# The vector engine's order in the first feed-forward layer: remainders of a later step, and reads of a finished product

## What is computed

```python
hn = rms_norm(h, p['norm_ff_g'])                      # h: 1280 x 1024
ff = jnp.square(jax.nn.relu(hn @ p['w_ff1'])) @ p['w_ff2']   # w_ff1: 1024 x 4096, w_ff2: 4096 x 1024
return h + ff
```

## Time and profile before

| | us |
|---|---|
| median of 3 runs | 2267.54 (2267.01 to 2267.8) |
| the profiled execution, its own time | 2268.52 |
| its span, from the first instruction to the last | 2266.8 |
| PE busy | 2212.8 (98% of the span) |
| PE weight loads busy | 1995.3 (88%) |
| DVE busy | 1438.4 (63%) |
| ACT busy | 1069.5 (47%) |

### The profile page before, as it was taken

How to read it: one execution, slowest core, us unless ns; L and a number is a source line. 1 busy time by engine, 2 the same in 40 slices (tenths; PEclk the granted TensorE clock), 3 DMA queues, 4 the chain that set the end, 5 groups by cost and what they waited for, 6 DMA issues and landing times.

```text
span 2266.8 us, 35228 instructions
## 1 busy us (share of the span) xinstructions
PE 2212.8 (98%) x13706; PEld 1995.3 (88%) x13706; DVE 1438.4 (63%) x2196; ACT 1069.5 (47%) x1870; POOL 166.0 (7%) x284
## 2 busy tenths in 40 slices
PE   8999999899998999999899999999999999999999
PEld 6888888788886888888788888899999999999999
DVE  6333455467653666677777645477676777786776
ACT  7533322266665444566633333365555654444442
POOL 0000000111100000000000000011111112111110
PEclk9999999999999999999999999999999999999999
DMA  4333322555545776888775243465555479887886
GB/s 163 109 118 135 114 95 81 143 137 158 137 126 161 237 229 220 264 260 264 229 256 168 87 157 106 150 208 195 177 200 195 159 249 355 297 288 251 275 289 235
DMA packets 227980, 434.92 MB, mean 192 GB/s; under 512 B 16355, under 2 KB 132963, under 8 KB 223116
## 3 DMA queue, kind: packets, MB, share of 16 engines
q1 hardware_dynamic: 188652, 321.71, 43.0%
q0 software_dynamic: 39200, 111.45, 16.2%
HBM read 331.93 MB, written 103.27 MB: 192 GB/s over the span
## 4 chain that ended last, share of the span: by engine, by line
PE 48%; DVE 2%; DMA 0%; issue 0%; ACT 0%; DVEq 0%
PE acc L150 13%; PE acc L148 13%; PE acc L149 13%; PE late_acc L148 3%; PE late_acc L149 3%; PE late_acc L150 3%; DVE xn_lo L1885 0%; DMA merged<-s_y_T 0%; DVE h_T L2597 0%; DVE hn_plain L2571 0%; DVE hn_plain L2580 0%; DVE ff_w_s L2588 0%; DVE gates L2006 0%; DVE ff_far_t_lo L2539 0%; DVE w_lo L2534 0%
## 5 line engine op out<-in xcount | busy, mean ns | idle before, releaser
L148 PE MATMUL acc<-xn_hi,w_hi 128*128 128x512 f32 (+1 forms) x1176 | 420.9, 358 | 22.8 <-DVE xn_lo L617 10.7
L149 PE MATMUL acc<-xn_hi,w_lo 128*128 128x512 f32 (+1 forms) x1176 | 418.4, 356 | 0.0
L150 PE MATMUL acc<-xn_lo,w_hi 128*128 128x512 f32 (+1 forms) x1176 | 417.6, 355 | 0.0
L148 PE MATMUL late_acc<-xn_hi,w_hi 128*128 128x512 f32 (+1 forms) x768 | 286.5, 373 | 3.0 <-DVE late_result_a L867 1.9
L148 PEld LDWEIGHTS acc<-xn_hi,w_hi 128*128 128x128 f32 x1176 | 223.5, 190 | 57.7 <-issue 13.6
L150 PE MATMUL late_acc<-xn_lo,w_hi 128*128 128x512 f32 (+1 forms) x768 | 274.2, 357 | 0.0
L149 PE MATMUL late_acc<-xn_hi,w_lo 128*128 128x512 f32 (+1 forms) x768 | 273.3, 356 | 0.0
L150 PEld LDWEIGHTS acc<-xn_lo,w_hi 128*128 128x128 f32 x1176 | 223.3, 190 | 31.6
L149 PEld LDWEIGHTS acc<-xn_hi,w_lo 128*128 128x128 f32 x1176 | 223.5, 190 | 31.2
L149 PE MATMUL acc<-ff_far_t_hi,w_lo 128*128 128x320 f32 x804 | 248.2, 309 | 0.0
L148 PEld LDWEIGHTS late_acc<-xn_hi,w_hi 128*128 128x128 f32 x768 | 146.3, 190 | 27.0 <-issue 6.6
(11 more groups left out here) (312 smaller groups left out, 4632.5 us busy)
## 6 DMA issues: line engine op xcount, KB each, us to landing
w_raw<-in_w_tiles SPq DMA_DIRECT2D x82, 512.0 KB, 4.2
ff_w_s<-in_w_ff SPq DMA_DIRECT2D x65, 512.0 KB, 6.4
gates<-s_t_ops POOLq DMA_DIRECT2D x86, 320.0 KB, 3.7
ff_part_q<-s_u_T POOLq DMA_DIRECT2D x33, 640.0 KB, 6.4
c_w<-s_ac SPq DMA_DIRECT2D x20, 1024.0 KB, 4.8
ff_part_v<-s_u_T POOLq DMA_DIRECT2D x31, 640.0 KB, 6.6
s_late_T<-late_result_s SPq DMA_DIRECT2D x20, 640.0 KB, 7.3
ff_w_a<-in_w_ff SPq DMA_DIRECT2D x12, 1024.0 KB, 6.0
```

The source lines that it names most:

```text
L148: pe.matmul(out, w_hi, x_hi, start=first, stop=False, skip_group_check=onto)
L149: pe.matmul(out, w_lo, x_hi, start=False, stop=False, skip_group_check=onto)
L150: return pe.matmul(out, w_hi, x_lo, start=False, stop=last, skip_group_check=onto)
```

## The change

In `vector`, the read of a finished product moves behind the two remainders of the same iteration, for all of DVE's products but the first (product 1, for which ACT's order above needs the old place). Fifteen reads move: products 4, 5, 6, 8, 11, 12, 13, 15, 18, 19, 20, 22, 25, 26 and 27. No instruction is added or removed, and no other engine's order changes.

```diff
             ended = self.ends(n, self.RING - 1) if n >= 7 else None
-            if ended is not None and not self.by_scalar(ended):
+            if ended == 1:
                 read(ended)
             if n < self.FIRST:
...
             else:
                 self.remainder_t(dve, n)
                 self.remainder_w(dve, n)
+            if ended is not None and ended > 1 and not self.by_scalar(ended):
+                read(ended)
             if n == 3:
                 self.out.mix(dve, 3)
             if self.FIRST <= n + 2 < self.STEPS:
```

## The result

| | before | after |
|---|---|---|
| median of 10 runs, us | 2268.66 (2267.01 to 2271.1) | 2274.87 (2272.19 to 2276.97) |
| profiled execution, us | 2268.52 | 2273.69 |
| its span, us | 2266.8 | 2271.8 |

The ratio is 1.0026 with a 95% interval from 1.0017 to 1.0036: the change costs 4 to 8 us, where 3.6 us was forecast and 2273.0 us was the top of the range. It is slower; whether by more than 0.2% the interval leaves open.

What follows compares the result with a forecast made beforehand. PE was taken to bound the kernel, with one 0.8 us wait for DVE. Steady reads 0.4 plus the second layer's start 3.2 made 3.6 us slower, forecast 2271.1 us (2270.2 to 2272.0); 8-in-10 range 2269.0 to 2273.0.

Steps and rivals of the forecast that it cites:

- What bounds the kernel: PE, at full clock, with one wait, before step 112; a new DVE order can win at most 0.8 us.
- Behind the turn: After step 112 starts late: no further cost, since DVE's 5.20 us idle before step 124's load covers the lateness.
- The steady reads: Thirteen put-off reads, products 4 to 25: bank 0 free 0.18 us ahead of need; 0.03 us each, 0.4 us.
- The turn, product 26 and product 27: Start of the second layer: DVE has no slack, so PE's idle time before step 112 grows by 3.18 us.
- own lateness of the moved read: Product 26: its read waits for step 111's remainders, so DVE is 0.57 us later at 1855.22.
- the two remainders: Product 27, iteration 115: its read stands behind `t_lo` and `w_lo`, 1.34 us, all on PE's path.
- The first load: POOL's load for step 114, issued after product 26's last read: takes 4.9 us, making DVE 1.84 us late.
- The load behind it: POOL's load for step 115, next after step 114's: the prediction counted no DVE wait for it.
- dear handovers: Rival: each of the 13 steady reads stalls PE 0.26 us or more; time 2274.3 to 2276.2 us; chance 0.15.
- the load is hidden: Rival: step 114's load lands within 3.6 us of issue; second layer's start costs 1.9 us, time 2269.8; chance 0.10.
- The turn doesn't close: Denies a rival: DVE runs through the second layer's start, PE's one wait goes, time 2266.7 us; chance 0.03.

Runs made afterwards that it cites:

- e8_early: Kernel before, with the read of product 27 one iteration earlier, behind step 114's remainders: 0.9992 of before (0.9983 to 1.0001), median 2267.31 us.
- product 27 alone: Kernel before, with only the read of product 27 put behind the remainders: 1.0011 of before (1.0002 to 1.0020).
- e2_steady: Kernel before, with only the thirteen reads of products 4 to 25 put behind the remainders: 1.0000 of before (0.9991 to 1.0009).
- e6_delay4: Kernel before, no read moved, four remainders computed in vain ahead of the read of product 27: 1.0025 of before (1.0016 to 1.0034).

## Why the prediction was wrong

**What bounds the kernel.** Right: PE, one wait, at step 112; no reordering could win more than 0.8 us, and in e8_early that wait is gone. One reading ahead of it was wrong: the clock line of the page doesn't say that the granted clock is full in every slice (see *Behind the turn*).

**The steady reads.** Right. For product 25 the bank's read was put 0.67 us ahead of its matmul; it came 0.68 us ahead. The loss is 0.02 us a product, within the bounds of 0 and 0.08.

**The turn, product 26 and product 27.** The own lateness of the moved read (0.57 forecast, 0.54 measured) and the two remainders (1.34 forecast; 1.32 with product 27 alone) were right. The first load was mis-sized: 4.9 us was taken, that of the same load before, and it landed after 4.2, so DVE waited 0.6 us from start to start and not 1.3. The runs point to the reason without an experiment of its own: SP's store of 1280 KB, issued 2.4 us ahead of this load in the kernel before and landing after 4.7 us, ran beside it there, and was issued 4.3 us ahead of it in the changed kernel. With 2.4 us between them the load took 4.7 to 4.9 us in the seven runs that leave the read of product 26 in its place; with 4.3 us it took 4.2 to 4.5 us in the four that put that read off and leave POOL's loads alone.

**The load behind it** is the first step whose mechanism failed. The prediction followed the put-off read into POOL's queue for one load and no further. The next load, for step 115, left later as well, and fell together with SP's load, which didn't move with it: SP's hangs on a remainder of DVE that stands ahead of DVE's waits. That made a second wait of 1.4 us. By the rows of before it would have been in time: it landed at 1861.25, 0.8 us ahead of its use at 1862.08, and load and DVE were both forecast some 1.9 us late. What it would meet on the way was not asked. With 0.65 us less for the first load and 1.42 us more for the second, the idle time came out at 4.7 us where 4.0 was forecast. The Trainium skill, DMA: Bandwidth & Descriptors, section "Issuing engines are not separate DMA queues", says that transfers issued by different engines run on the same 16 DMA engines and interleave; the 6.1 and 4.5 us with and without SP's load agree.

**Behind the turn** is the step that put the time outside the range. "I cost the rest at nothing" priced PE's idle time at its length. In the changed kernel the granted clock fell behind it, and 1.5 us came on top. The forecast had read the clock from the page's 40 slices, where a 9 stands for 90% or more of a slice of 57 us and hides a few us at half clock. The trace of before had the warning, far ahead of the change, where PE had waited 1.94 us for a DVE instruction (stretches, as above):

```profile
411.40:413.30 1.90, 0.05 (x1) 0.00 (x0) 0.66 (x2) 0.38 (x1) 0.17 (x1) 1.00 0.00 0
...
414.80:418.10 3.30, 3.30 (x17) 3.20 (x16) 0.61 (x2) 0.00 (x0) 2.36 (x4) 0.50 1.16 276
```

Elsewhere in that trace the clock is at 0.50 or 0.51 behind PE's waits of 2.14, 3.35, 4.39 and 8.56 us too, and full behind those of 1.57 to 1.74 us. With an idle time of 4 us ahead and these rows read, some 1.5 us more belonged into the sum, and the forecast would have been 2272.6 us. The Trainium skill, TensorE: Matmul & The Clock Gate, section "HAM oscillation — how this bites in real kernels", describes a kernel whose waits for loads let PE's clock fall, so that the next work starts at half speed each time; the 4.22 us of pure delay (e6_delay4) agree.

**The sum against the median.** Forecast 0.4 + 3.2 = 3.6; in the profiled execution 0.3 + 3.9 + 1.5 = 5.7 us. The medians differ by 6.2 us, which the interval of 3.9 to 8.2 us doesn't tell from 5.7. The forecast stood on a median of before of 2267.54 us from three runs; ten have 2268.66, and that is a further 1.1 us of the distance. Two figures of the prediction miss its own sums by 0.2 to 0.3 us: 2267.54 + 2.9 is 2270.4, not 2270.2, and dear handovers with 3.2 us for the turn make 2274.1 to 2275.9, not 2274.3 to 2276.2. Nothing hangs on them.

**The rivals.** That the load is hidden is out, by DVE's wait for it. Dear handovers are out by e2_steady; the kernel got slower by some 0.26%, but not for that reason. The turn doesn't close by the change; it closes when the read is taken earlier (e8_early).

## What to carry to other kernels

Where an engine that is free for most of the time runs without a gap just ahead of the bounding engine's wait, every instruction put in front of the awaited one counts in full, however idle that engine is on average. Follow each release that moves through all loads that stand behind it in the same queue, and ask what other queue's transfers they now meet. An idle time of TensorE of a few us may cost more than its length: read the granted clock behind such waits in a view by short stretches, since a page in slices doesn't show it.

## What the runs showed of the hardware that was not expected

Behind an idle time of 2.1 to 4.7 us the granted clock was at 1.2 GHz in six profiled executions, at a loss of 1.5 us in three of them and 2.2 to 2.5 us in the other three, where the half clock lasted longer (from the start of step 112 to the last matmul, against before); in two others, behind 2.51 and 3.04 us, it stayed at 2.4 GHz. A load of 640 KB issued by POOL took 4.5 or 6.1 us depending on whether a load of 512 KB was issued by SP 0.2 us later, and the later one overtook it (4.0 us against 9.6). And POOL let 2.25 us pass between two loads with nothing to wait for, at the same place in the program in the kernels before and after, right ahead of the load for step 115 that came late; the profile calls it issue, and the runs don't say why.
